# Expert products in column halves, output stores a step later, and a closing pass with all gathers issued at once

## What is computed

```python
def hier_moe(h, lp):                       # h: 512 tokens x 1024
    ...                                    # router: 4 groups x 4 experts, top 2 in the best group
    for e in range(N_EXPERTS):             # 16 experts of width 512
        a = jax.nn.silu(h @ lp['w_gate'][e]) * (h @ lp['w_up'][e])
        y = y + combine[..., e, None] * (a @ lp['w_down'][e])

h2 = modulate(rmsnorm(x, g_pre_ffn[l]), shift2, scale2)
x = x + gate2 * rmsnorm(hier_moe(h2, lp), g_post_ffn[l])
```

## Time and profile before

| | |
|---|---|
| three runs, median (lowest to highest) | 2074.79 us (2074.19 to 2078.51) |
| the profiled execution | 2073.45 us |
| its span, first to last instruction | 2072.0 us |
| one block of the expert loop | 20.14 us |
| first gate matmul to the last expert output stored | 1653.3 to 2027.8 us |
| first closing gather to the end | 2028.8 to 2072.0 us |
| DVE, ACT, PE busy in a block of 20.14 us | 16.98, 15.48, 18.58 us |

### The profile page before, as it was taken

One profiled execution on the slowest core, in us unless ns is written; L12 is line 12 of the kernel. 1 busy time (PEld: TensorE's weight loads), 2 busy tenths in 40 slices (PEclk: granted clock), 3 DMA queues, 4 the chain that ended last, 5 costly groups with the idle time before them and its releaser, 6 DMA issues.

```text
span 2072.0 us, 24514 instructions
## 1 busy us (share of the span) xinstructions
PE 1820.4 (88%) x8710; PEld 1488.0 (72%) x8710; DVE 1227.8 (59%) x2145; ACT 874.9 (42%) x1382; POOL 109.5 (5%) x132
## 2 busy tenths in 40 slices
PE   8897899999998977899999997999687299999982
PEld 7776788888887656788888886866577277777762
DVE  3555668885226555568665226455733388888874
ACT  3346532233215446332323214335622177777761
POOL 1000000000000000001100001000000201001001
PEclk9899899999998989999999997999885599999996
DMA  4323235454331240246543333202110499999963
GB/s 141 94 69 118 62 102 142 133 148 129 100 100 44 71 183 11 71 113 190 163 134 111 102 93 98 82 1 72 51 41 8 166 343 369 361 361 368 359 249 132
DMA packets 224050, 294.57 MB, mean 142 GB/s; under 512 B 13344, under 2 KB 151560, under 8 KB 223832
## 3 DMA queue, kind: packets, MB, share of 16 engines
q1 hardware_dynamic: 205492, 235.36, 34.8%
q0 software_dynamic: 12080, 41.65, 6.4%
q10 hardware_dynamic: 6388, 16.35, 2.1%
HBM read 271.78 MB, written 21.54 MB: 142 GB/s over the span
## 4 chain that ended last, share of the span: by engine, by line
PE 78%; DVE 10%; ACT 7%; issue 2%; DMA 2%; POOL 0%; DVEq 0%; ACTq 0%; POOLq 0%; SPq 0%
PE bank L200 23%; PE bank L202 22%; PE bank L201 22%; PE bank L69 11%; DVE tmp L69 2%; DVE weights_low L227 1%; DMA out_second<-slot_output,pair_slots 1%; ACT weights_high L221 1%; ACT squares L69 1%; DVE z_and_u L69 1%; DVE hidden_low L2287 1%; DVE expert_hidden L2275 1%; PE bank L2280 1%; ACT hidden_high L2285 1%; PE bank L272 0%
## 5 line engine op out<-in xcount | busy, mean ns | idle before, releaser
L227 DVE TENSOR_TENSOR weights_low<-ring,weights_high 128x1024 fp32r<-128x1024 f32 x202 | 246.7, 1223 | 407.4 <-ACT weights_high L221 407.3
L200 PE MATMUL bank<-XH,weights_high 128*128 128x512 f32 x1120 | 454.0, 405 | 30.0 <-DVE XL L69 20.3
L202 PE MATMUL bank<-XH,weights_low 128*128 128x512 f32 x1120 | 444.0, 396 | 0.0
L201 PE MATMUL bank<-XL,weights_high 128*128 128x512 f32 x1120 | 443.3, 396 | 0.0
L221 ACT CAST weights_high<-ring 128x1024 fp32r<-128x1024 f32 x202 | 211.1, 1047 | 439.3 <-PE bank L202 438.2
L200 PEld LDWEIGHTS bank<-XH,weights_high 128*128 128x128 f32 x1120 | 215.4, 192 | 78.7 <-ACT squares L69 12.3
L202 PEld LDWEIGHTS bank<-XH,weights_low 128*128 128x128 f32 x1120 | 214.7, 192 | 47.1
L201 PEld LDWEIGHTS bank<-XL,weights_high 128*128 128x128 f32 x1120 | 215.3, 192 | 42.8 <-issue 0.5
L2211 DVE TENSOR_TENSOR XL<-ring,XH 128x1024 fp32r<-128x1024 f32 x144 | 169.7, 1220 | 31.0 <-ACT XH L2209 31.0
L2209 ACT CAST XH<-ring 128x1024 fp32r<-128x1024 f32 x144 | 143.5, 1046 | 0.0
L69 DVE SCALAR_TENSOR_TENSOR squares<-ring,c_silu,squares 128x128 f32<-128x128 f32 x384 | 135.2, 352 | 13.6
(11 more groups left out here) (445 smaller groups left out, 2953.6 us busy)
## 6 DMA issues: line engine op xcount, KB each, us to landing
ring<-in_w_ffn_in SPq DMA_DIRECT2D x88, 512.0 KB, 4.7
ring<-in_w_gate SPq DMA_DIRECT2D x72, 512.0 KB, 4.9
ring<-in_w_up SPq DMA_DIRECT2D x72, 512.0 KB, 8.5
ring<-in_w_down SPq DMA_DIRECT2D x72, 512.0 KB, 10.5
ring<-in_w_ada POOLq DMA_DIRECT2D x48, 512.0 KB, 4.7
ring<-in_w_ffn_out SPq DMA_DIRECT2D x44, 512.0 KB, 3.5
ring<-in_w_out SPq DMA_DIRECT2D x24, 512.0 KB, 3.5
slot_output<-expert_out SPq DMA_DIRECT2D x18, 512.0 KB, 3.8
```

The lines of the kernel that those rows point to most:

```text
L200: PE.matmul(out_ap, w_h, x_h, start=first, stop=False, skip_group_check=True)
L201: PE.matmul(out_ap, w_h, x_l, start=False, stop=False, skip_group_check=True)
L202: return PE.matmul(out_ap, w_l, x_h, start=False, stop=last, skip_group_check=True)
L227: V.tensor_tensor(wl[:, s, :], ring[s][:, :], wh[:, s, :].bitcast(F32), ALU.subtract).then_inc(split_done.sem, 1)
```

## The change

1. **Up in halves.** Each 512-column up matmul becomes two of 256 columns, one in bank 1 and one in bank 7. For unit 7 the first half is finished before the second begins. `av`, the four transposes, `ath` and `atl` are done half by half. Down units 8 and 9 wait for the first half of `atl`, unit 10 for the second. `turn_rows` stands between the two half transposes on PE.
2. **Stores later.** SP stores block b-1's result inside block b, between the fetches of the next block's gate and up units, so its loop turns without waiting for the result. `yd` gets a row block more, slot numbers are 128 higher, the first store holds zeros (a DVE memset that SP waits for), and the last result has a store of its own.
3. **Output copies.** ACT makes both; DVE's is gone.
4. **End.** Buffers for all four groups; eight gathers issued back to back; the first weighting on ACT; scale and epsilon inside the root; the sqrt table loaded ahead; stores in column halves on SP. The residual's transposes and the gain row are made in the router, by PE and ACT, and kept in SBUF.
5. **Router.** `seq` waits for DVE's own last operation, and for ACT or PE only where named.

The diff, cut to its core:

```diff
+        def token_rows():
+            for t4 in range(TT):
+                for half in range(2):
+                    b = 2 + (2 * t4 + half) % 6
+                    pe.need(*bank_free[b])
+                    for c in range(4):
+                        k = 4 * half + c
+                        t = pe.do(PE.transpose, bank[b][:, c * P:(c + 1) * P], X[:, k, t4 * P:(t4 + 1) * P], ident)
+                    bank_free[b] = [act.do(S.copy, x_tok[:, t4, half * 512:(half + 1) * 512], bank[b][:, :], after=[t])]
...
-            return vec.do(op, *args, after=[vec.line.now(), act.line.now(), pe.line.now()], **kw)
+            return vec.do(op, *args, after=[vec.line.now(), *after], **kw)
...
+        for half in range(2):
+            b = 6 + half
+            pe.need(*bank_free[b])
+            for c in range(4):
+                k = 4 * half + c
+                t = pe.do(PE.matmul, bank[b][:, c * P:(c + 1) * P], POST_FFN[:, k:k + 1].broadcast_to([P, P]), ident,
+                          start=True, stop=True)
+            bank_free[b] = [act.do(S.copy, grow[:, half * 512:(half + 1) * 512], bank[b][:, :], after=[t])]
+
+        token_rows()
+        seq(V.tensor_copy, cnt[:, :], bank[1][:, TT * NE:(TT + 1) * NE], after=[counted])
...
+            seq(V.tensor_scalar, slots_u[:, j, :], g1[:, :, 0], float(P), None, ALU.add)
...
+        sp.need(vec.do(V.memset, yt[:, :], 0.0))
...
-                for q in range(UNITS):
+                for q in range(4):
+                    fetch(b + 1, e, q)
+            reach(SP, l_y0, b)
+            reach(SP, l_y1, b)
+            SP.dma_start(yd[bass.ds(b * P, P), :], yt[:, :]).then_inc(l_st.sem, 16)
+            if not last:
+                for q in range(4, UNITS):
                     fetch(b + 1, e, q)
...
+            def up(q, halves, c):
+                s, k = q % HELD, 2 * (q - 4) + c
+                for n in halves:
+                    cols = slice(c * DE + n * 256, c * DE + (n + 1) * 256)
+                    t = three_pass(bank[(1, 7)[n]][:, 0:256], hgh[:, k, :], hgl[:, k, :], high[s][:, cols],
+                                   low[s][:, cols], k == 0, k == KC - 1)
+                return t
+            def hidden(n):
+                if n == 0:
+                    reach(V, l_up, b + 1)
+                    reach(V, l_silu, b + 1)
+                    reach(V, l_at, b * 2)
+                else:
+                    reach(V, l_used, b * UNITS + 8)
+                V.tensor_tensor(av[:, n * 256:(n + 1) * 256], sg[:, n * 256:(n + 1) * 256], bank[(1, 7)[n]][:, 0:256],
+                                ALU.mult).then_inc(l_av.sem, 1)
+            def hidden_turn(n):
+                reach(PE, l_av, b * 2 + (n + 1))
+                for k in range(2 * n, 2 * n + 2):
+                    t = PE.transpose(bank[(6, 1)[n]][:, (k % 2) * P:(k % 2 + 1) * P], av[:, k * P:(k + 1) * P], ident)
+            def hidden_split(n):
+                src = bank[(6, 1)[n]][:, 0:256].rearrange("p (k n) -> p k n", k=2)
+                dst = slice(2 * n, 2 * n + 2)
+                reach(S, l_at, b * 2 + (n + 1))
+                S.copy(ath[:, dst, :], src).then_inc(l_ath.sem, 1)
+                reach(V, l_ath, b * 2 + (n + 1))
+                V.tensor_tensor(atl[:, dst, :], src, ath[:, dst, :].bitcast(F32), ALU.subtract).then_inc(l_atl.sem, 1)
...
+            for q in range(4, 7):
+                split_ahead(q)
+                wait_split(PE, b, q)
+                up(q, (0, 1), 0)
+                up(q, (0, 1), 1).then_inc(l_used.sem, 1)
+            wait_split(PE, b, 7)
+            up(7, (0,), 0)
+            up(7, (0,), 1).then_inc(l_up.sem, 1)
+            up(7, (1,), 0)
+            up(7, (1,), 1).then_inc(l_used.sem, 1)
+            hidden(0)
+            hidden(1)
+            hidden_turn(0)
+            if not last:
+                turn_rows(b + 1)
+            hidden_turn(1)
+            hidden_split(0)
+            hidden_split(1)
             split_ahead(7)
-            reach(PE, l_atl, b + 1)
+            reach(PE, l_atl, b * 2 + 1)
...
+                if q == 10:
+                    reach(PE, l_atl, b * 2 + 2)
+                down(q)
...
-            V.tensor_copy(yt[:, 512:1024], bank[3][:, :]).then_inc(l_y1.sem, 1)
+            S.copy(yt[:, 512:1024], bank[3][:, :]).then_inc(l_y1.sem, 1)
...
+        root_table()
+        for t4 in range(TT):
+            for j, dst in enumerate((first, second)):
+                G.indirect_dma_start(dst[:, t4, :], None, yd,
+                                     bass.IndirectOffsetOnAxis(ap=slots_u[:, j, t4:t4 + 1], axis=0)).then_inc(
+                    l_pair[t4].sem, 16)
+        def pair_sum(t4):
+            t = act.do(S.activation, first[:, t4, :], first[:, t4, :], ACT.Copy, scale=wts[:, 0, t4:t4 + 1],
+                       after=[l_pair[t4].now()])
+            summed[t4] = vec.do(V.scalar_tensor_tensor, first[:, t4, :], second[:, t4, :], wts[:, 1, t4:t4 + 1],
+                                first[:, t4, :], ALU.mult, ALU.add, after=[t])
+            t = act.do(S.activation, second[:, t4, :], first[:, t4, :], ACT.Square, accum_out=ss[:, t4:t4 + 1],
+                       after=[summed[t4]])
+            t = act.do(S.activation, root[:, t4:t4 + 1], ss[:, t4:t4 + 1], ACT.Sqrt, scale=1.0 / D,
+                       bias=epsilon[:, 0:1], after=[t])
+        def finish_tokens(t4, rooted):
+            t = vec.do(V.reciprocal, root[:, t4:t4 + 1], root[:, t4:t4 + 1], after=[rooted])
+            scaled[t4] = vec.do(V.scalar_tensor_tensor, first[:, t4, :], first[:, t4, :], root[:, t4:t4 + 1], grow[:, :],
+                                ALU.mult, ALU.mult, after=[t])
+            for half in range(2):
+                t = vec.do(V.tensor_tensor, first[:, t4, cols], first[:, t4, cols], x_tok[:, t4, cols], ALU.add,
+                           after=[scaled[t4]])
+                load(sp, lout, out[0, t4 * P:(t4 + 1) * P, cols], first[:, t4, cols], after=[t])
+        rooted = pair_sum(0)
+        for t4 in range(1, TT):
+            following = pair_sum(t4)
+            finish_tokens(t4 - 1, rooted)
+            rooted = following
+        finish_tokens(TT - 1, rooted)
```

More of the change, by code:

```diff
@@ L2023, in sm, with seq @@
             return small[name]
-        def seq(op, *args, **kw):
-            return vec.do(op, *args, after=[vec.line.now(), act.line.now(), pe.line.now()], **kw)
+        def seq(op, *args, after=(), **kw):
+            return vec.do(op, *args, after=[vec.line.now(), *after], **kw)
         def bc(ap, *shape):
@@ L2053, in program @@
         seq(V.tensor_tensor, e4[:, :, :], lg[:, :, 0:4], bc(m1[:, :, :], TT, 4), ALU.subtract)
-        act.do(S.activation, e4[:, :, :], e4[:, :, :], ACT.Exp, after=[vec.line.now()])
-        seq(V.tensor_reduce, psel[:, :, 0], e4[:, :, :], AX, ALU.add)
+        t = act.do(S.activation, e4[:, :, :], e4[:, :, :], ACT.Exp, after=[vec.line.now()])
+        seq(V.tensor_reduce, psel[:, :, 0], e4[:, :, :], AX, ALU.add, after=[t])
         seq(V.reciprocal, psel[:, :, :], psel[:, :, :])
@@ L2065, in program @@
         seq(V.tensor_tensor, m2[:, :, :], m2[:, :, :], m1[:, :, :], ALU.subtract)
-        act.do(S.activation, m2[:, :, :], m2[:, :, :], ACT.Exp, after=[vec.line.now()])
-        seq(V.tensor_scalar, m1[:, :, :], m2[:, :, :], 1.0, None, ALU.add)
+        t = act.do(S.activation, m2[:, :, :], m2[:, :, :], ACT.Exp, after=[vec.line.now()])
+        seq(V.tensor_scalar, m1[:, :, :], m2[:, :, :], 1.0, None, ALU.add, after=[t])
         seq(V.reciprocal, m1[:, :, :], m1[:, :, :])
@@ L2257, in block, with down @@
+            def down(q):
+                s, k = q % HELD, q - 8
+                wait_split(PE, b, q)
+                for n in range(2):
+                    t = three_pass(bank[2 + n][:, :], ath[:, k, :], atl[:, k, :], high[s][:, n * 512:(n + 1) * 512],
+                                   low[s][:, n * 512:(n + 1) * 512], k == 0, k == 3)
+                t.then_inc(l_used.sem, 1)
+            if not last:
+                gather(b + 1)
             reach(S, l_table, b)
@@ L2262, in block @@
                 split_ahead(q)
-                wide(q)
+                gate(q)
             reach(S, l_used, b * UNITS + 4)
-            reach(S, l_av, b)
+            reach(S, l_av, b * 2)
             S.activation(sg[:, :], bank[0][:, :], ACT.Silu).then_inc(l_silu.sem, 1)
[L2267 to L2283, removed]
+            reach(PE, l_av, b * 2)
+            for q in range(4, 7):
+                split_ahead(q)
+                wait_split(PE, b, q)
+                up(q, (0, 1), 0)
[8 more added lines that the diff above has]
+            hidden_turn(0)
+            if not last:
+                turn_rows(b + 1)
+            hidden_turn(1)
             reach(S, l_used, b * UNITS)
-            S.copy(ath[:, :, :], src6).then_inc(l_ath.sem, 1)
-            reach(V, l_ath, b + 1)
-            V.tensor_tensor(atl[:, :, :], src6, ath[:, :, :].bitcast(F32), ALU.subtract).then_inc(l_atl.sem, 1)
```

(14 more changed lines are left out.)

83 lines of the change are left out of this document (31 added, 52 removed).

## The result

The changed kernel takes 2045.72 us (median of four runs, 2045.18 to 2049.57) against 2074.49 (2070.95 to 2078.51) of the kernel before on the same chip: a ratio of 0.9865, 95% interval 0.9843 to 0.9886, so 24 to 33 us faster. The forecast was 2051 with a range from 2042 to 2062.

The account below looks back on a forecast made before the run. PE led the old loop with one stall; the ACT and DVE ring would set the new pace, 19.6 us a block. Loop -9.5, last block -0.2, ending -14.6, router +0.5 make -23.8: 2074.8 to 2051, range 2042 to 2062.

Parts of the forecast that it names:

- PE led before, and the halves shorten its stall: Loop, between up and down: PE's stall of 3.47 us falls to 1.68; led by PE, a block takes 18.5.
- rival 3: Up matmuls: 256 columns held to their weight load's 0.19, about +3.5 us a block, whole 2120; 4%.
- The ACT and DVE ring takes the lead at 19.6: Loop: copies, table load, casts, low parts, product, transposes sum to 19.62 us a block; gain 9.5 over 17 blocks.
- PE's wait of about 0.6 for the gathered rows: Loop, block start: first gate matmul waits about 0.6 us because DVE splits the gathered rows' second half late.
- Stores a step later: Loop, SP's output store moved into the next block: gate fetches move earlier and fill a hole; cost nothing.
- Transfers as a floor of 18.8: Loop's DMA: demand 0.97 over full stretches' 1.04, times 20.14, allows no block under 18.8 us.
- the rule of about 358 GB/s: HBM limit a core: the loop would already stand there and gain none of 9.5 us; forecast held it inapplicable.
- The last block: -0.2: Last block: halves save about 0.5 us, the second copy on ACT delays the last store by 0.3.
- the gain that the forecast kept for its range: Last block's down matmuls: another 2.4 us if the shorter stall keeps PE's full clock; left out of the sum.
- The ending: -14.6: First closing gather to end: 28.6 us instead of 43.2, DVE leading from 11.3 to 26.2, then the last half store.
- rival 4: Ending: eight queued gathers slow each other, pairs land 5 us apart, end 2 to 4 us later, 2054; 9%.
- Router: +0.5: Router: 0.5 us charged for transfers now beside the scatters, bounds 0 and 2; lighter `seq` waits save nothing visible.

Follow-up runs that it names:

- experiment 9: Probe: changed kernel plus one more ScalarE copy of 512 columns into a tile nobody reads, ahead of the second output copy; 2053.65 us.
- experiment 1: Changed kernel with the second output copy moved back to VectorE; 2039.1 us, period 19.27.
- experiment 3: Changed kernel with both ScalarE output copies made in the next block, ahead of its first hidden cast, and the store moved with them; 2040.31 us.
- experiment 4: Changed kernel with late ScalarE output copies and their store, and gathered rows split ahead of the weight unit in down units 8 and 9; 2034.22 us.
- experiment 5: Changed kernel with the output store taken back to the end of the block; 2043.35 us, period 19.53.
- experiment 6: Changed kernel with GpSimd waiting in the ending until each pair of gathers has landed; 2056.13 us, ending 37.15.
- experiment 2: Changed kernel with full-width up products, one product, four transposes and one split behind them; 2066.65 us, period 20.35.
- experiment 8: The kernel of experiment 4 unchanged, timed again; 2028.14 us median of five runs, ratio 0.977 to the kernel before.
- experiment 10: The kernel of experiment 4 plus one more ScalarE copy of 512 columns into a tile nobody reads; 2029.03 us.
- experiment 7: Changed kernel's router and ending around the loop and slot numbers of the kernel before; 2061.59 us, period 20.13 to 20.15.

## Why the prediction was right

**PE led before, and the halves shorten its stall.** Shown. With the copies as in the change, halves or full width differ by 0.82 a block, and the stall's rows come and go with them. The 256-column matmuls start 0.12 apart, as the earlier trace rows had it: PE's busy time rose by only 0.15 a block, and rival 3 is out.

**The ACT and DVE ring takes the lead at 19.6.** Shown, by the brackets, by the ring's own rows that add up to 19.53, and by the probe that it passes on in full. The forecast's links were right to 0.03 each but for one: transposes and passage 1.56 instead of 1.64. That is most of the 0.09 between 19.62 and 19.53. The loop gave 10.64 instead of 9.5: 9.24 in the 15 blocks in the middle, 1.28 in the first, of which 0.32 is only a shorter stretch at the low clock, and 0.12 in the last step, from one gate to that of the last block. The copy's 0.48 is only half of what lengthens the ring from 18.67 to 19.62. The rest is the second half's cast, which stands behind the next rows' transposes (1.64 against 0.69), less what the halves save. Other orders of these transposes were not tried.

**PE's wait of about 0.6 for the gathered rows.** Measured 0.57. The forecast took it for a consequence only. Experiments 1 and 3 end at about 19.3 with that wait in place, and experiment 4 removes both: it closes a loop of its own just below the ring.

**Stores a step later: nothing.** Shown by experiment 5.

**Transfers as a floor of 18.8.** Without effect on the sum, and a little too high: the loop of experiment 4 runs at 18.66. Its share column reads 1.04 over those 14 blocks, so the transfers are now nearly as full as TensorE. Still PE, DVE, ACT and GpSimd show no wait on a landing in that window, so a floor of theirs was not reached here and its place stays open. The loop moves 394 GB/s on average. Of the rule of about 358 GB/s that the forecast weighed: the Trainium skill, HBM Reference, "Specifications (TRN2)", gives that figure for both cores of a pair streaming and about 425 for a core alone. One core ran here, and its 394, a pace set by TensorE and not by the transfers, lie between the two; no run here had the neighbour busy.

**The last block: -0.2.** This is the term that was mis-sized: -3.07. One microsecond of it is the passage from the end of the last up matmul to the first down one, which took 3.68 before and 2.66 after (2011.51 to 2015.19, 2004.22 to 2006.88), where the forecast saved 0.5. Another 1.07 is a wait of PE at its first up matmul, for the low part of unit 4, that the changed kernel has not. The timeline at the start of the last block, first before, then changed:

```profile
1998.66 0.50 PE L200 MATMUL bank<-weights_high,gathered_high 128*128 128x512 f32 x1
...
2001.89 1.28 ACT L2258 ACT_TABLE_LOAD   x1 [2.55 <-issue]
...
2005.64 0.50 PE L200 MATMUL bank<-XH,gathered_high 128*128 128x512 f32 x1 [1.12 <-DVE XL L2211]
```

```profile
1992.44 0.49 PE L200 MATMUL bank<-weights_high,gathered_high 128*128 128x512 f32 x1 [1.16 <-DVE gathered_low L2209]
...
1994.55 1.28 ACT L2337 ACT_TABLE_LOAD   x1 [1.92 <-issue]
```

Before, PE began this block at once, and ACT's casts came late behind an idle time of 2.55. Afterwards PE already waits 1.16 at its first gate matmul, against 0.57 inside the loop, and ACT idles 0.63 less. So about 0.6 of the 1.07 has only moved into the stage before, where the last step gained just 0.12. The forecast had no row for any of this. The last 0.98 is in the down products, whose time depends on the granted clock: the gain that the forecast kept for its range. Of the 3.07, then, 1.0 is shown to be the shorter passage; the rest hangs on the clock and on ACT's idle time.

**The ending: -14.6.** Measured -14.51, of which experiment 6 separates the gathers' 8.45. The first pair landed 6.67 after the first gather (6.4 forecast), DVE led from 11.93 on (11.3) and was done with its adds at about 26.5 (26.2); the last store then took 2.2, at the lower end of its bounds, which makes the sum look closer than its links. The pairs landed 2.6 to 3.0 apart, the last at 15.0, and no later landing showed, so rival 4 fell.

**Router: +0.5.** Measured +0.76. The first scatter goes out 15.47 after the first counting product in both kernels, so the lighter waits of `seq` save nothing. GpSimd then waits longer for two landings: 2.06 instead of 1.45 for the scatters, 3.80 instead of 3.59 for the slots' tokens. That fits the transfers that the forecast charged; no run tries it by itself.

## What to carry to other kernels

- Near a balanced bound, add up the links of the ring that would follow the one you shorten. Here 0.27 us of slack told beforehand that a work item of 0.48 moved to a 77% busy engine would cost time: the 0.21 left over in experiment 2.
- An engine's busy share doesn't say whether it has room. A dummy instruction in the place in question does, and it costs one run: here it was passed on in full on the ring and vanished beside it. Taking work out tells less, because the next loop may stand just below (0.26 for 0.48 in experiment 1).
- Where a change pays, look at what waits next. Moving the two copies to where their engine waits anyway and splitting first what is needed first gave some 17 us more.

## What the runs showed of the hardware

**The granted clock of the last down products differs between executions of nearly the same code.** PE idles about as long before them in the changed kernel and in experiment 5 (1.22 and 0.67, 1.27 and 0.67), yet they get different clocks. The changed kernel, the first and fourth of 24 down matmuls and the windows row over them:

```profile
2006.88 0.50 PE L200 MATMUL bank<-XH,hidden_high 128*128 128x512 f32 x1 [0.67 <-DVE hidden_low L2323]
...
2007.75 0.63 PE L200 MATMUL bank<-XH,hidden_high 128*128 128x512 f32 x1
```

```profile
2007.00:2014.40 7.40, 7.28 (x24) 5.46 (x24) 1.30 (x2) 0.58 (x2) 0.00 (x0) 0.77 0.00 0
```

Experiment 5, the same products:

```profile
2001.63 0.49 PE L200 MATMUL bank<-XH,hidden_high 128*128 128x512 f32 x1 [0.67 <-DVE hidden_low L2316]
2001.96 0.39 PE L201 MATMUL bank<-XL,hidden_high 128*128 128x512 f32 x1
```

In the first the clock falls to 1.2 GHz at the fourth matmul, and eight of them start 0.43 apart. In the second all keep 2.4 GHz, 0.23 apart. From the first to the end of the last the 24 take 7.40 and 5.85 us; in the kernel before, with some twelve at the low clock, 8.45. They kept the full clock in experiments 1, 3, 4, 5, 8, 9 and 10 and lost it for a while in 2, 6 and 7; experiment 6 has the changed kernel's loop, experiment 5 too but for the store. What decides it stays open. One such stretch is worth 1.5 to 2.6 us in these comparisons of single executions. The loop's first gate products are another: they begin at 1.2 GHz in all twelve profiled executions, and the 24 of them take from 6.97 us (experiment 7) to 8.51 (experiment 5).

**Behind the device loop ScalarE can idle for 1.5 to 2.6 us with no releaser in the trace.** In the changed kernel's last block the table load stands 1.92 behind the copies with no releaser but "issue"; inside the loop it stands 0.02 behind them. The kernel before has 2.55 there, and the other kernels with the copies in this place 1.47 to 2.55. In experiments 3, 4, 8 and 10, whose copies stand elsewhere, it is 0.21 to 0.27. What makes it is not shown. The root's table load at the start of the ending, 2.95 behind its copies, also reads "issue" but is another thing: it starts at 2018.41, 0.05 after the landing of the last output store, for which the kernel waits.
